# The layers' dense columns as three products of rounded parts

## The chip, the cores and the metric

The program runs on one core of a Trainium2 chip. The metric is the time of one execution on the device, in microseconds (us). Five engines take part: TensorE (PE; its weight loads are rows of their own, PEld), VectorE (DVE), ScalarE (ACT), GpSimd (POOL) and SyncE (SP), which issues nearly all the transfers from memory (DMA).

## What is computed

The reference is two layers of one model, a final norm, and then a block of a second model, all in fp32 with 256 tokens of 1024 features. The change concerns the two layers, and there the products of the normed tokens with columns of `w_in`:

```python
for layer in range(DEPTH):                      # DEPTH = 2
    h = rms_norm(x, norm1_g[layer])             # 256 x 1024
    sb = cols(SB_OFF, SB_COLS)                  # cols: h @ w_l[:, lo:lo + width]
    y_sb = stick_breaking_attention(...)
    y_rwkv, v_first = rwkv7_time_mix(cols(RWKV_OFF, RWKV_COLS), ...)
    y_moba = moba_attention(...)                # of cols(MOBA_OFF, MOBA_COLS)
    y_hgrn = hgrn2_mixer(...)                   # of cols(HGRN_OFF, HGRN_COLS)
    for n, y_n in enumerate((y_sb, y_rwkv, y_moba, y_hgrn)):
        gate = jax.nn.sigmoid(cols(GATE_OFF + n * D_MODEL, D_MODEL))
        merged += gate * (y_n @ w_branch[layer, n])
    x = x + merged @ w_out[layer]
    h2 = rms_norm(x, norm2_g[layer])
    x = x + (silu(h2 @ w_ffn_gate[layer]) * (h2 @ w_ffn_up[layer])) @ w_ffn_down[layer]
```

The columns are 768 for `sb`, 768 for `moba`, 1024 for `hgrn` and 4096 for the four gates; the 1024 of `rwkv` are computed before the others and aren't changed. They are 6656 columns a layer.

## The kernel before

Everything is written by hand: each engine has a program of its own, and semaphores order them. A tile is 128 partitions wide, so the 1024 features are 8 tiles of 128 x 256 (`x`, `B.h`).

**A unit** is what one visit to a PSUM bank makes: 128 columns for all 256 tokens (kind "c"), or 256 columns for 128 tokens (kinds "0" and "1", for the values of the attentions). It is 8 products, of 128x128 with 128x256, in fp32; the profile shows each fp32 product as two matmul rows. A layer has 52 units: 20 for the branches (`hq`, `hg`, `sq`, `sv`, `mq`, `mv`), then 32 for the gates. The generator `units` stops after every 4 products, so a unit is two half-units and a layer has 104.

**The order in a layer.** First come the RWKV columns (the loop over `RP`, matmuls of L1145), while VectorE makes the normed tiles `h` and the shifted `R.p`. Then the RWKV recurrence runs in 42 steps, each a few small matmuls with work of VectorE or ScalarE between them. `mix` puts half-units between the steps: `RW_PLAN` says how many follow each one (7, 3, 1, 4, 3, then mostly 1; 64 in all). The matmuls of these steps are those of L743 and L739 and some of L212, those of the units are L212 with `ring` among their operands. Steps on which the prediction rests: "kn" (the norm of the keys: VectorE makes `kk2`, PE sums, VectorE makes `kmax`, ScalarE takes Ln and Exp with two table loads, VectorE makes `rk` for the next step "bo"); "wc/we" (PE, then three exponentials on ScalarE, then VectorE makes `AR` and `KB`, then PE transposes `KB`); four steps M with one for L (VectorE masks what PE made); 24 steps that double an inverse in six levels; five steps of W, U and y; and the norm of `y`, whose variance VectorE makes, whose root ScalarE makes, and which PE transposes ("yT"). Then the branch product `b1`, and then the steps of `hgrn`, `stick` and `moba` by turns, with the other 40 half-units between them by `MX_PLAN`. After that PE does the other branch products, the output product (L1173) and the feed-forward part.

All engines run the same `mix` with the same plan, and each engine executes its own program strictly in order. On ScalarE the half-units are where it empties the bank of the unit before:

```python
for i in range(n):
    yield
    if i:
        done(i - 1)
    yield
```

**Loads.** SyncE fills three slots of 16 KB a partition in turn (`ring`); a slot is free when PE has used what was in it. Before the change a slot takes 512 columns (2048 KB) or 256 (1024 KB).

**The feed-forward part** (`split`, `group3`) already works in the way that the change brings to the units: ScalarE copies fp32 weights rounded to fp32r (`high_part`), VectorE subtracts that from the weights to make the low part (`low_part`), and PE makes three products in fp32r (high by high, high by low, low by high) in place of one in fp32. Its operands are named `rarena`.

Of the kernel before, what the change touches and what calls it, by code (L numbers as in the profile page):

```python
# [6 lines left out]
ALU = mybir.AluOpType  # L7
# [6 lines left out]
L = 2  # L14
# [6 lines left out]
IN1 = 7680  # L21
# [246 lines left out]
def build(nc, a, outs, coff, ooff, ocols):  # L268
    with ExitStack() as ctx:
# [9 lines left out]
        ring = ctx.enter_context(nc.sbuf_tensor("ring", [128, NSLOT, SLOT], F32))  # L279
# [62 lines left out]
        def pc(key, i=0, n=1):  # L342
# [40 lines left out]
        B.h = alloc(8, 256)  # L383
        B.tm = alloc(2, 256)
# [7 lines left out]
        B.hg = alloc(2, 256)  # L392
        mark = place["top"]
        R = Space()
        R.rp = alloc(8, 257)
        R.p = alloc(8, 256)
        R.r, R.k, R.v = R.p[:, 0:2, :], R.p[:, 2:4, :], R.p[:, 4:6, :]
        R.th = alloc(256)
        R.lw = alloc(2, 256)
        R.av = alloc(2, 256)  # L400
        R.sg = alloc(256)
        R.g = alloc(2, 256)
        R.M4 = alloc(8, 512)
        mm_ = flat(R.M4)
        R.vv = mm_[:, 0:256]
        R.vg = halves(mm_[:, 256:768])
        R.dv = halves(mm_[:, 768:1280])
        R.kk = alloc(2, 256)
# [7 lines left out]
        R.KB = alloc(2, 2, 256)  # L416
        R.em = alloc(2, 2)
# [8 lines left out]
        R.Wt = alloc(256)  # L426
        R.U = alloc(256)
# [4 lines left out]
        H = Space()  # L432
        H.key = alloc(2, 256)
        H.lf = alloc(2, 256)
        H.qd = alloc(2, 256)
# [123 lines left out]
        IN1 = [("hq", 2560, 512, "cccc"), ("hg", 3072, 512, "01cc"), ("sq", 0, 512, "cccc"), ("sv", 512, 256, "01"),  # L559
               ("mq", 1792, 512, "cccc"), ("mv", 2304, 256, "01")]  # L560
        gate_col = lambda n, ch: 3584 + 1024 * n + 512 * ch
# [50 lines left out]
        def sync_program(S):  # L612
# [19 lines left out]
            def units(l, c0, w, n):  # L632
                columns(f"{l}w{c0}", a["w_in"][l], 8, c0, w)
                for _ in range(n):
                    yield
                    yield

            def proj(l):
                for nm, c0, w, parts in IN1:
                    yield from units(l, c0, w, len(parts))  # L640

            def gate(l, n, ch):
                yield from units(l, gate_col(n, ch), 512, 4)
# [15 lines left out]
            for l in range(L):  # L659
# [8 lines left out]
                fill = [proj(l)] + [gate(l, n, ch) for n in (1, 0, 2, 3) for ch in range(2)]  # L668
# [49 lines left out]
        def tensor_program(PE):  # L718
# [31 lines left out]
            def units(l, nm, c0, w, parts):  # L750
                wt = halves(wslot(f"{l}w{c0}")[:, 0:8 * w], 8)
                PE.wait_ge(f"{l}w{c0}")
                o = 0
                for i, kind in enumerate(parts):
                    b = take("p", f"{l}{nm}{i}.ps", f"{l}{nm}{i}.out")
                    if kind == "c":
                        out = b[:, 0:256]
                        prs = [(wt[:, j, o:o + 128], B.h[:, j, :]) for j in range(8)]
                        o += 128
                    else:  # L760
                        t = int(kind)
                        out = b[:, 0:256]
                        prs = [(B.h[:, j, 128 * t:128 * t + 128], wt[:, j, o:o + 256]) for j in range(8)]
                        o += 256 if t == 1 else 0
                    PE.group(out, prs[0:4], end=False)
                    yield
                    PE.group(out, prs[4:8], first=False).then_inc(*PE(f"{l}{nm}{i}.ps"))
                    yield
                PE.mark(f"{l}w{c0}.used")

            def proj(l):
                for nm, c0, w, parts in IN1:
                    yield from units(l, nm, c0, w, parts)

            def gate(l, n, ch):
                yield from units(l, f"g{n}{ch}", gate_col(n, ch), 512, "cccc")
# [2211 lines left out]
```

## Time and profile before

| | us |
|---|---|
| median of 3 runs (lowest to highest) | 1977.25 (1975.52 to 1977.47) |
| the profiled execution, by its own time | 1975.95 |
| its span in the trace | 1974.2 |
| in it, first layer, from the first unit to the last step of the mixers | 42.6 to 315.8 |
| the same stretch of the second layer | 620.7 to 896.3 |

The profile is one execution. In the views below a time is in us from the start of the span. "idle" in a row is how long the engine stood before it, with what released it. TensorE is busy nearly everywhere in the two layers; the last quarter of the span, the second model's experts, waits for transfers. The granted clock of TensorE is a share of its full speed, 1.00 being 2.4 GHz and 0.50 being 1.2 GHz.

### The profile page before, as it was taken

To read this page: it belongs to the slowest core of one execution; us is meant where nothing else is said; L and a number is where in the kernel's file an instruction comes from. 1 tells how busy PE (TensorE), PEld (TensorE's weight loads), DVE (VectorE), ACT (ScalarE), POOL (GpSimd) and SP (SyncE) were. 2 spreads that over 40 slices of the span, in tenths; PEclk is the share of its full clock that TensorE was granted. 3 is DMA by queue.
4 is the path that set the end of the run, shared out by engine and by line. 5 is a ranking of instruction groups with operands and counts; after the bars stand their busy time and mean duration, and the time that the engine had idled before them with its cause. 6 is when DMAs were issued, how large, how long until landed. Compare 5 with 4: busy or idle time off the path is not lost.

```text
span 1974.2 us, 25562 instructions
## 1 busy us (share of the span) xinstructions
PE 1782.2 (90%) x11030; PEld 1388.9 (70%) x11030; DVE 746.4 (38%) x1220; ACT 513.6 (26%) x776; POOL 36.5 (2%) x42
## 2 busy tenths in 40 slices
PE   8999999999999999999999999999998975656655
PEld 6899887988898898888999998567887321111111
DVE  4532435455434532425666666332345100000001
ACT  2201221544342101211544464432542100000001
POOL 0000000100010000000100020000000000000000
PEclk9999999999999999999999999999999988888888
DMA  7221323677834221315554331401229999999997
GB/s 305 76 104 71 156 76 121 244 308 302 326 118 149 79 114 64 150 65 201 218 191 179 133 117 49 168 1 43 86 86 377 426 428 426 428 428 426 428 427 312
DMA packets 31073, 414.82 MB, mean 210 GB/s; under 512 B 3440, under 2 KB 3696, under 8 KB 4336
## 3 DMA queue, kind: packets, MB, share of 16 engines
q1 hardware_dynamic: 30528, 410.63, 52.2%
q10 hardware_dynamic: 432, 2.56, 0.3%
q8 instruction: 86, 1.41, 0.3%
q14 instruction: 27, 0.22, 0.0%
HBM read 412.13 MB, written 1.05 MB: 209 GB/s over the span
## 4 chain that ended last, share of the span: by engine, by line
PE 79%; DMA 15%; DVE 2%; ACT 1%; another core or an unknown queue 1%; issue 1%; POOL 0%; SPq 0%; DVEq 0%; ACTq 0%
PE ps L212 56%; DMA high<-in_w_e_gate_dram 7%; PE ps L743 7%; DMA high<-in_w_e_up_dram 5%; PE ps L1530 4%; PE ps L1145 3%; PE ps L1173 3%; DMA low<-in_w_e_up_dram 2%; PE ps L787 1%; DVE high L171 1%; ACT high L206 1%; PE ps L739 1%; PE ps L1545 1%; PE ps L1419 1%
## 5 line engine op out<-in xcount | busy, mean ns | idle before, releaser
L212 PE MATMUL ps<-high,ring 128*128 128x256 f32 (+1 forms) x2016 | 471.7, 386 | 0.9 <-ACT low L206 0.9
L212 PEld LDWEIGHTS ps<-rarena 128*128 128x128 f32 x3648 | 447.6, 192 | 16.3 <-DVE low L171 6.9
L212 PE MATMUL ps<-rarena 128*128 128x256 f32 (+1 forms) x3648 | 457.8, 287 | 0.0
L212 PEld LDWEIGHTS ps<-high,ring 128*128 128x128 f32 x2016 | 375.0, 190 | 65.6 <-issue 15.4
L206 ACT ACTIVATE high<-ps 128x256 f32<-128x256 f32 (+2 forms) x188 | 90.9, 483 | 623.3 <-PE ps L212 220.6
L171 DVE TENSOR_TENSOR rarena<-ring,rarena 128x2048 fp32r<-128x2048 f32 x76 | 168.4, 2215 | 106.9 <-ACT rarena L206 105.5
L206 ACT ACTIVATE rarena<-ring 128x2048 fp32r<-128x2048 f32 x76 | 140.4, 1847 | 243.5 <-PE ps L212 189.0
L171 DVE TENSOR_TENSOR high<-high,ps 128x512 f32<-128x512 f32 x52 | 35.7, 687 | 305.1 <-PE ps L1530 247.3
L1530 PE MATMUL ps<-high,low 128*32 128x512 f32 x592 | 90.1, 736 | 50.6 <-DMA high<-in_w_e_up_dram 33.8
L743 PEld LDWEIGHTS ps<-high 128*128 128x128 f32 (+1 forms) x992 | 104.0, 190 | 16.6 <-issue 8.0
L743 PE MATMUL ps<-high 128*128 128x128 f32 (+4 forms) x992 | 113.1, 291 | 1.9 <-DVE high L171 1.9
L206 ACT ACTIVATE low<-ps 128x256 f32<-128x256 f32 (+2 forms) x97 | 43.5, 448 | 267.7 <-PE ps L212 207.8
L212 PE MATMUL ps<-high 128*128 128x64 f32 (+5 forms) x512 | 111.5, 368 | 0.8 <-DVE high L193 0.8
L212 PEld LDWEIGHTS ps<-high 128*128 128x128 f32 (+2 forms) x512 | 83.5, 190 | 24.4 <-issue 13.4
L171 DVE TENSOR_TENSOR high<-ps,low 128x512 f32<-128x512 f32 (+1 forms) x47 | 30.1, 640 | 181.6 <-PE ps L1530 140.0
L1530 PEld LDWEIGHTS ps<-high,low 128*32 128x32 f32 x592 | 17.8, 122 | 112.5 <-DMA high<-in_w_e_up_dram 56.2
L171 DVE TENSOR_TENSOR high<-high 128x256 f32<-128x256 f32 (+9 forms) x108 | 59.1, 548 | 77.2 <-PE ps L743 53.7
L1530 PE MATMUL ps<-high 128*32 128x512 f32 x272 | 43.1, 764 | 31.4 <-DMA high<-in_w_e_down_dram 30.2
L1145 PE MATMUL ps<-low,ring 128*128 128x256 f32 x256 | 60.0, 394 | 8.6 <-DMA ring<-in_w_in_dram 8.6
L212 PE MATMUL ps<-low,ring 128*128 128x256 f32 x264 | 62.1, 395 | 4.5 <-issue 4.5
L206 ACT ACT_TABLE_LOAD x46 | 59.0, 1283 | 16.3 <-DVE high L176 13.3
L1145 PEld LDWEIGHTS ps<-low,ring 128*128 128x128 f32 x256 | 50.2, 198 | 16.9 <-DMA ring<-in_w_in_dram 8.6
(188 smaller groups left out, 1439.0 us busy)
## 6 DMA issues: line engine op xcount, KB each, us to landing
ring<-in_w_in_dram SPq DMA_DIRECT2D x34, 2048.0 KB, 7.5
ring<-in_w_ffn_up_dram SPq DMA_DIRECT2D x22, 2048.0 KB, 9.2
high<-in_w_e_up_dram SPq DMA_DIRECT2D x20, 2048.0 KB, 49.6
high<-in_w_e_gate_dram SPq DMA_DIRECT2D x17, 2048.0 KB, 47.7
high<-in_w_e_down_dram SPq DMA_DIRECT2D x17, 2048.0 KB, 50.4
ring<-in_w_mod_dram SPq DMA_DIRECT2D x12, 2048.0 KB, 8.2
ring<-in_w_e_down_dram SPq DMA_DIRECT2D x10, 2048.0 KB, 48.7
ring<-in_w_ffn_down_dram SPq DMA_DIRECT2D x8, 2048.0 KB, 8.4
```

Of the source, the lines that this page charges most:

```text
L171: return self.e.tensor_tensor(out, x, y, op)
L206: return self.e.activation(out, x, f, scale=scale, **kw)
L212: ins = self.e.matmul(out, l, r, start=first and i == 0, stop=end and i == n - 1)
L739: ins = PE.e.transpose(o, z, ident[0:k, 0:k])
L743: return PE.e.matmul(out, l, r, start=True, stop=True)
L787: ins = PE.e.matmul(b[32 * j:32 * j + 2, :], cc[:, 2 * kq + k, :], w[:, k, j, :], start=kq == 0 and k == 0, stop=kq == 3 and k == 1)
L1145: ins = PE.e.matmul(b[:, 0:256], w[:, j, 128 * m:128 * m + 128], B.xg[:, j, :], start=j == 0, stop=j == 7)
L1173: ins = PE.e.matmul(b[:, 0:256], w[:, j, 128 * m:128 * m + 128], B.mg[:, j, :], start=j == 0, stop=j == 7)
L1419: ins = PE.e.matmul(bs[i][:, 0:256], w[:, k, 128 * i:128 * i + 128], T.yT[:, k, :], start=k == 0, stop=k == 7)
L1530: ins = PE.e.matmul(bs[ch][32 * e_:32 * e_ + 32, :], lhs(k, e_), w[:, e_, 512 * ch:512 * ch + 512], start=k == 0, stop=k == 7)
L1545: ins = PE.e.matmul(banks[4 + 2 * t + ch][:, :], E.SGT[:, g_, 128 * t:128 * t + 128], E.y[:, 512 * ch:512 * ch + 512], start=g_ == 0, stop ...
```

## The change

Both operands of the units are split. `B.h` is rounded by ScalarE to `B.hh` and VectorE makes the rest, `B.hl`. Of the weights, ScalarE rounds the columns of one unit, two units ahead of its use, into the upper half of the slot (`high_weights`); GpSimd subtracts and writes the low part over the weights (`low_weights`); PE waits for GpSimd and makes three fp32r products where one fp32 product was. A load brings 256 columns, two units. The buffers of RWKV are laid over one another to make room (`R.p`, `R.th`, `R.lw` and others lie in `R.M4`), and those of hgrn move in front of them. The loads of the RWKV columns, the feed-forward part and everything after the layers stay.

```diff
@@ -276,7 +276,9 @@
-        ring = ctx.enter_context(nc.sbuf_tensor("ring", [128, NSLOT, SLOT], F32))
+        with nc.sbuf_tensor("ring", [128, NSLOT, SLOT], F32) as ring:
+            pass
+        rring = ctx.enter_context(nc.sbuf_tensor("rring", [128, NSLOT, SLOT], mybir.dt.float32r))
...
@@ -381,6 +383,8 @@
+        place["top"] -= 8 * 256
+        B.hl, B.hh = ralloc_low(8, 256), ralloc_low(8, 256)
...
         R.M4 = alloc(8, 512)
         mm_ = flat(R.M4)
+        R.p = mm_[:, 0:2048].rearrange("p (i n) -> p i n", i=8)
+        R.r, R.k, R.v = R.p[:, 0:2, :], R.p[:, 2:4, :], R.p[:, 4:6, :]
+        R.th, R.sg = mm_[:, 2048:2304], mm_[:, 2304:2560]
+        R.lw, R.av, R.kk = (halves(mm_[:, o:o + 512]) for o in (2560, 3072, 3584))
+        R.g = alloc(2, 256)
...
+        R.vg, R.dv = R.KB[:, 0, :, :], R.KB[:, 1, :, :]
...
+        GATES = [(f"g{n}{ch}", 3584 + 1024 * n + 512 * ch, "cccc") for n in (1, 0, 2, 3) for ch in range(2)]
+        UNITS = [(nm, i, kind, c0 + 256 * (i // 2), i % 2) for nm, c0, kinds in IN1 + GATES for i, kind in enumerate(kinds)]
+        raw_part = lambda ld: halves(wslot(ld)[:, 0:2048], 8)
+        rslot = lambda ld: rring[:, slot_of.get(ld, 0), :].bitcast(F32)
+        low_weights = lambda ld: halves(rslot(ld)[:, 0:2048], 8)
+        high_weights = lambda ld: halves(rslot(ld)[:, 2048:4096], 8)
+        unit_columns = lambda z: slice(128 * z, 128 * z + 128)
...
+            def units(l):
+                for nm, i, kind, c0, z in UNITS:
+                    if z == 0:
+                        columns(f"{l}w{c0}", a["w_in"][l], 8, c0, 256)
+                    yield
+                    yield
...
@@ -747,33 +747,23 @@
+            def units(l):
+                for u, (nm, i, kind, c0, z) in enumerate(UNITS):
+                    wl, wh = low_weights(f"{l}w{c0}"), high_weights(f"{l}w{c0}")
+                    PE.wait_ge(f"{l}u{u}.lo" if kind == "c" else f"{l}u{u + 1 - z}.lo")
...
                     if kind == "c":
-                        out = b[:, 0:256]
-                        prs = [(wt[:, j, o:o + 128], B.h[:, j, :]) for j in range(8)]
-                        o += 128
+                        o = unit_columns(z)
+                        prs = [(wh[:, j, o], wl[:, j, o], B.hh[:, j, :], B.hl[:, j, :]) for j in range(8)]
+                        o = unit_columns(int(kind))
+                        prs = [(B.hh[:, j, o], B.hl[:, j, o], wh[:, j, :], wl[:, j, :]) for j in range(8)]
+                    PE.group3(b[:, 0:256], prs[0:4], end=False)
+                    yield
+                    PE.group3(b[:, 0:256], prs[4:8], first=False).then_inc(*PE(f"{l}{nm}{i}.ps"))
+                    if z:
+                        PE.mark(f"{l}w{c0}.used")
+                    yield
...
-                PE.wait_ge(f"{l}h7")
-                fill = [proj(l)] + [gate(l, n, ch) for n in (1, 0, 2, 3) for ch in range(2)]
...
+            def gate_unit(l, nm, i):
...
+            def rounded(l, u):
+                nm, i, kind, c0, z = UNITS[u]
+                A.wait_ge(f"{l}w{c0}")
+                o = unit_columns(z)
+                high_part(f"{l}u{u}.hi", high_weights(f"{l}w{c0}")[:, :, o], raw_part(f"{l}w{c0}")[:, :, o])
+
+            def rounded_ahead(l, u):
+
+                kind, z = UNITS[u][2], UNITS[u][4]
+                if kind == "c":
+                    rounded(l, u)
+                elif z == 0:
+                    rounded(l, u)
+                    rounded(l, u + 1)
+
+            def units(l):
+                for u in range(len(UNITS)):
+                    yield
+                    if u:
+                        nm, i = UNITS[u - 1][0:2]
+                        (gate_unit if nm[0:2] in ("g0", "g1", "g2", "g3") else input_unit)(l, nm, i)
+                    if u + 2 < len(UNITS):
+                        rounded_ahead(l, u + 2)
+                    yield
+                gate_unit(l, *UNITS[-1][0:2])
...
                 for n in range(8):
+                    A.wait_ge(f"{l}h{n}")
+                    high_part(f"{l}h{n}.hi", B.hh[:, n, :], B.h[:, n, :])
                     if n in EARLY_STEPS[l]:
                         next(rw)
-                fill = [proj(l)] + [gate(l, n, ch) for n in (1, 0, 2, 3) for ch in range(2)]
+                rounded(l, 0)
+                rounded(l, 1)
...
+                def normed_tile(n):
+                    V.stt(B.h[:, n, :], x[:, n, :], pc(("norm1_g", l), n), B.rs, mul, mul).then_inc(*V(f"{l}h{n}"))
+
+                def low_tile(n):
+                    V.wait_ge(f"{l}h{n}.hi")
+                    low_part(B.hl[:, n, :], B.h[:, n, :], B.hh[:, n, :], f"{l}h{n}.lo")
+
+                normed_tile(0)
                 for n, i in enumerate(RP):
-                    V.stt(B.h[:, n, :], x[:, n, :], pc(("norm1_g", l), n), B.rs, mul, mul).then_inc(*V(f"{l}h{n}"))
+                    if n < 7:
+                        normed_tile(n + 1)
+                    low_tile(n)
                     V.wait_ge(f"{l}rp{i}.ps")
...
+            def units(l):
+                for u, (nm, i, kind, c0, z) in enumerate(UNITS):
+                    G.wait_ge(f"{l}u{u}.hi")
+                    raw, o = raw_part(f"{l}w{c0}"), unit_columns(z)
+                    G.tt(fr(low_weights(f"{l}w{c0}")[:, :, o]), raw[:, :, o], high_weights(f"{l}w{c0}")[:, :, o], ALU.subtract).then_inc(
+                        *G(f"{l}u{u}.lo"))
...
+    out["w_in"] = [column_blocks(w["w_in"][l], [256, 256, 256, 512] + 25 * [256]) for l in range(L)]
```

`raw` in the program of GpSimd is `raw_part`, the fp32 weights in the slot.

ScalarE's queue from the last tile of `h` over the step "kn" (table load, 128x512, table load, 128x512 are its Ln and Exp) to the first emptied banks (`high<-ps 128x256`); `rring<-ring` is the rounding of one unit:

```order
+L206 ACTIVATE rarena<-high 128x256
+L206 ACTIVATE rring<-ring 128x8x128 x2
 L206 ACT_TABLE_LOAD
 L206 ACTIVATE high<-high 128x512
 L206 ACT_TABLE_LOAD
 L206 ACTIVATE high<-high 128x512
-L206 ACTIVATE high<-ps 128x256 x2
+L206 ACTIVATE rring<-ring 128x8x128
+L206 ACTIVATE high<-ps 128x256
+L206 ACTIVATE rring<-ring 128x8x128
+L206 ACTIVATE high<-ps 128x256
+L206 ACTIVATE rring<-ring 128x8x128 x2
```

Two roundings (of units 0 and 1) stand ahead of the Ln and Exp of "kn", and the third (of unit 2) stands behind them.

TensorE's queue from the last RWKV column (L1135, before L1145) over "kn" (the first L743 128x512) and "bo" (the second); an order row counts an fp32 product once:

```order
-L1145 MATMUL ps<-low,ring 128x256 x8
-L212 MATMUL ps<-high,ring 128x256 x8
+L1135 MATMUL ps<-low,ring 128x256 x8
+L212 MATMUL ps<-rarena,rring 128x256 x24
 L743 MATMUL ps<-high,low 128x512
-L212 MATMUL ps<-high,ring 128x256 x20
+L212 MATMUL ps<-rarena,rring 128x256 x60
 L743 MATMUL ps<-high,low 128x512
```

The units stand where they stood, with three matmuls for one; unit 0 is ahead of "kn", and units 1, 2 and half of 3 are between "kn" and "bo".

GpSimd's queue between the sums for the first layer's two norms:

```order
-L171 TENSOR_TENSOR low<-low 128x256 x29
+L171 TENSOR_TENSOR low<-low 128x256
+L171 TENSOR_TENSOR rring<-ring,rring 128x8x128 x52
+L171 TENSOR_TENSOR low<-low 128x256 x14
+L171 TENSOR_TENSOR rring<-ring,rring 128x8x128 x52
+L171 TENSOR_TENSOR low<-low 128x256 x14
```

It gets 52 subtractions of 128x1024 in each layer.

## Rows read from the trace of the kernel before

**Rows 1.** The page, first part: busy time by engine.

```profile
PE 1782.2 (90%) x11030; PEld 1388.9 (70%) x11030; DVE 746.4 (38%) x1220; ACT 513.6 (26%) x776; POOL 36.5 (2%) x42
```

**Rows 2.** Windows: busy us of PE, PEld, DVE, ACT, POOL, clock, DMA.

```profile
100.00:200.00 100.00, 100.00 (x633) 91.79 (x632) 31.90 (x55) 9.59 (x21) 0.00 (x0) 1.00 0.25 92
```

**Rows 3.** Timeline, first layer, around "kn": start, us, engine, operation, count, idle before.

```profile
42.57 3.62 PE L212 MATMUL ps<-high,ring 128*128 128x256 f32 x16
45.44 0.69 DVE L171 TENSOR_TENSOR high<-high 128x512 f32<-128x512 f32 x1
47.15 8.80 PE L212 MATMUL ps<-high,ring 128*128 128x256 f32 x40
48.11 1.28 ACT L206 ACT_TABLE_LOAD   x1 [8.20 <-DVE high L176]
52.01 0.69 DVE L171 TENSOR_TENSOR high<-high 128x512 f32<-128x512 f32 x1 [3.96 <-ACT high L206]
54.36 1.01 DVE L181 SCALAR_TENSOR_TENSOR high<-high,col 128x256 f32<-128x256 f32 x2
55.79 1.02 PE L743 MATMUL ps<-high,low 128*128 128x512 f32 x2
```

**Rows 4.** Timeline of PE in the feed-forward part (fp32r, two jobs of 48).

```profile
385.15 11.78 PE L212 MATMUL ps<-rarena 128*128 128x256 f32 x96
396.86 1.90 PE L787 MATMUL ps<-ring,low 128*2 128x512 f32 x16
```

**Rows 5.** Groups by line and shape: busy us, mean ns | idle before.

```profile
L171 POOL TENSOR_TENSOR low<-low 128x1024 f32<-128x1024 f32 x1 | 2.3, 2342 | 9.8 <-ACT low L206 9.8
...
L206 ACT ACTIVATE rarena<-ring 128x1024 fp32r<-128x1024 f32 x6 | 6.4, 1060 | 17.7 <-PE ps L212 17.6
...
L171 DVE TENSOR_TENSOR rarena<-high,rarena 128x256 fp32r<-128x256 f32 x8 | 3.7, 468 | 1.4 <-ACT high L206 0.7
```

**Rows 6.** DMA issues: KB each, median us to landing.

```profile
ring<-in_w_in_dram SPq DMA_DIRECT2D x8, 1024.0 KB, 4.9
```

**Rows 7.** Timeline, second layer, around the first unit.

```profile
620.74 3.72 PE L212 MATMUL ps<-high,ring 128*128 128x256 f32 x16
620.84 0.98 ACT L206 ACTIVATE high<-ps,low 128x256 f32<-128x256 f32 x2 [8.54 <-PE ps L743]
```

**Rows 8.** Timeline, first layer, "wc/we" to M.

```profile
65.54 2.74 ACT L206 ACTIVATE high<-ps 128x512 f32<-128x512 f32 x5 [6.58 <-PE ps L743]
69.01 2.60 DVE L171 TENSOR_TENSOR high<-high 128x256 f32<-128x256 f32 x4
72.03 1.01 PEld L739 LDWEIGHTS ps<-cst,high 128*128 128x128 f32 x8
78.39 1.14 PE L743 MATMUL ps<-high 64*128 64x256 f32 x8
```

**Rows 9.** Timeline, first layer, the end of the M stage.

```profile
98.14 1.16 PE L743 MATMUL ps<-high 128*128 128x128 f32 x8 [0.68 <-DVE high L171]
```

**Rows 10.** Timeline: a GpSimd operation beside one of VectorE, four places.

```profile
360.83 2.29 DVE L171 TENSOR_TENSOR rarena<-ring,rarena 128x2048 fp32r<-128x2048 f32 x1
360.86 2.84 POOL L171 TENSOR_TENSOR low<-low 128x256 f32<-128x256 f32 x1 [346.13 <-ACT low L206]
...
364.72 0.72 POOL L171 TENSOR_TENSOR low<-low 128x256 f32<-128x256 f32 x1 [1.01 <-ACT low L206]
364.81 0.42 DVE L181 SCALAR_TENSOR_TENSOR low<-ps,low 128x256 f32<-128x256 f32 x1
...
1158.38 0.73 POOL L171 TENSOR_TENSOR high<-high 128x256 f32<-128x256 f32 x1
1158.61 0.79 DVE L181 SCALAR_TENSOR_TENSOR low<-low 128x256 f32<-128x256 f32 x1 [3.61 <-ACT low L206]
```

**Rows 11.** Timeline and windows, the end of the first layer's fill.

```profile
318.09 3.65 PE L212 MATMUL ps<-low,ring 128*128 128x256 f32 x8 [2.27 <-issue]
...
318.50:319.00 0.50, 0.50 (x2) 0.39 (x2) 0.00 (x0) 0.00 (x0) 0.00 (x0) 0.50 0.00 0
```

More of the change, by code:

```diff
@@ L392, in build @@
         B.hg = alloc(2, 256)
+        H = Space()
+        H.key = alloc(2, 256)
+        H.lf = alloc(2, 256)
+        H.qd = alloc(2, 256)
         mark = place["top"]
@@ L426, in build @@
         R.Wt = alloc(256)
+        R.vv = R.Wt
         R.U = alloc(256)
@@ L431, in build @@
         gx = [B.gates] + [alloc(8, 256) for _ in range(2)]
[L432 to L435, printed above, removed]
         H.ST = alloc(8, 128)
@@ L667, in sync_program @@
                     table["par"] = (s_par, 32)
-                fill = [proj(l)] + [gate(l, n, ch) for n in (1, 0, 2, 3) for ch in range(2)]
+                fill = [units(l)]
                 mix([none(RW_STEPS)], fill, RW_PLAN, False)
@@ L1153, in tensor_program @@
                         next(rw)
-                PE.wait_ge(f"{l}h7")
-                fill = [proj(l)] + [gate(l, n, ch) for n in (1, 0, 2, 3) for ch in range(2)]
+                PE.wait_ge(f"{l}h7.lo")
+                fill = [units(l)]
                 for _ in range(2):
@@ L1609, in input_unit @@
                     evict(l, nm, i, B.mv[:, i, :])
[L1611 to L1626 removed]
+            def gate_unit(l, nm, i):
+                n, ch = int(nm[1]), int(nm[2])
+                buf = B.mg if n == 1 else gx[max(n - 1, 0)]
+                evict(l, nm, i, buf[:, 4 * ch + i, :], Tanh, scale=0.5)
+            def rounded(l, u):
[12 more added lines that the diff above has]
+                for u in range(len(UNITS)):
+                    yield
+                    if u:
[3 more added lines that the diff above has]
+                        rounded_ahead(l, u + 2)
+                    yield
+                gate_unit(l, *UNITS[-1][0:2])
             def none(n):
@@ L1809, in scalar_program @@
                 for n in range(8):
+                    A.wait_ge(f"{l}h{n}")
+                    high_part(f"{l}h{n}.hi", B.hh[:, n, :], B.h[:, n, :])
                     if n in EARLY_STEPS[l]:
                         next(rw)
-                fill = [proj(l)] + [gate(l, n, ch) for n in (1, 0, 2, 3) for ch in range(2)]
+                rounded(l, 0)
+                rounded(l, 1)
+                fill = [units(l)]
                 mix([rw], fill, RW_PLAN, False)
@@ L2075, in proj @@
             def proj(l):
-                for nm, c0, w, parts in IN1[:2]:
-                    yield from late(len(parts), lambda i, nm=nm: input_unit(l, nm, i))
+                for nm, c0, kinds in IN1[:2]:
+                    yield from late(len(kinds), lambda i, nm=nm: input_unit(l, nm, i))
             def modulation():
@@ L2801, in pool_program @@
             G.mark("0n1.fold")
+            units(0)
             folded("0n2", F.sq)
             folded("1n1", B.gates)
+            units(1)
             folded("1n2", F.sq)
@@ L2883, in pack_weights @@
     out = {}
-    out["w_in"] = [column_blocks(w["w_in"][l], [512, 256, 512, 256, 256, 512, 256] + 10 * [512]) for l in range(L)]
+    out["w_in"] = [column_blocks(w["w_in"][l], [256, 256, 256, 512] + 25 * [256]) for l in range(L)]
     out["w_branch"] = [[rows_on_partitions(w["w_branch"][l, n], 2) for n in range(4)] for l in range(L)]
```

52 lines of the change are left out of this document (2 added, 50 removed).

## The prediction

> **What bounds the kernel now.** I read the page first: TensorE is busy 90% of the span, GpSimd 2% [rows 1]. The windows of 100 us say the same of the layers: from 100 to 200 TensorE is busy all of the time at clock 1.00, VectorE a third of it and ScalarE a tenth [rows 2]. So the layers last as long as TensorE's queue, and the other engines work in its shade. How deep the shade is, the timeline shows. At the step "kn", VectorE's last operation ends at 46.13, TensorE then gives 5 half-units (47.15 to 55.79) while ScalarE's Ln and Exp with two table loads run to 52.01 and VectorE finishes `rk` at 55.37, 0.4 us before TensorE asks for it [rows 3]. In this place cover and chain are equally long. That is where I look for losses.
>
> **What TensorE saves.** Five fp32 half-units take 55.79 - 47.15 = 8.64, so one takes 1.728 [rows 3]. In the feed-forward part 96 fp32r matmuls take 396.86 - 385.15 = 11.71, or 0.122 each; a half-unit of 12 will take 1.464 [rows 4]. The difference is 0.264, and 2 layers x 104 half-units give **-54.9 us**, if nobody makes TensorE wait.
>
> **What is added.** For each unit ScalarE rounds 128x1024 (1.06) and GpSimd subtracts 128x1024 (2.34; this row is of a plain tile, the new one is read in 8 runs) [rows 5]. A unit on TensorE will take 2.93, so in steady state both keep up; 52 x 2.34 = 122 us of GpSimd a layer lie under some 270. VectorE's eight low tiles (0.47 each) lie in the RWKV columns, where it waits for TensorE anyway: nothing, and 3.7 a layer without that cover. Their roundings on ScalarE (8 x 0.5) lie there too. The laid-over buffers cost nothing: what shares `R.M4` is read before the first M in each queue. Loads of 1024 KB land in 4.9 [rows 6]; a slot is refilled while two units (5.9 or more) run, so they arrive in time, with 1 us to spare in a run of units without steps. A miss would cost under 1 us at each of a few loads; I count none.
>
> What isn't free is the order. A unit needs, one after the other, ScalarE's rounding and GpSimd's subtraction: 1.06 + 2.34 and hand-overs, 3.5. ScalarE does that two units ahead, but behind what its queue holds.
>
> 1. First unit. In the first layer the roundings follow the last tile of `h`; I get 1.4 us of waiting by the same sum. In the second, ScalarE is at the attention to `vg` until 620.84 + 0.98 = 621.82, so unit 0 is ready at 625.3, where TensorE wanted it at 620.74: 4.6 [rows 7]. Together **+6.0**.
> 2. Unit 2 at "kn". The queue has its rounding behind Ln and Exp. ScalarE begins these 2.0 after `kk2` (48.11 against 46.13) and ends them 3.9 later [rows 3]; with 3.5 behind it unit 2 is ready 9.4 after TensorE begins "kn". TensorE has only "kn" (1.0) and unit 1 (2.93) until then: 5.5 in each layer, **+11.0**. This is what the old cover hid: all five half-units could run under ScalarE's work, now two can.
> 3. In the rest of the burst (18 half-units up to M) the same happens smaller: pairs of units "01" wait for the second low part, and unit 7's rounding stands behind the three exponentials of "wc/we", whose result TensorE's transposes need too (from 65.54 to 72.03, of which four half-units now cover 5.9) [rows 8]: 2 a layer, **+4.0**.
> 4. M stage. From 78.39 to 98.14 VectorE has no pause to speak of, and TensorE waits for it at the end [rows 8, 9]. Its 7 faster half-units gain nothing: 7 x 0.264, **+3.7**. In the 24 steps of the doubling VectorE has 0.5 to 1 us to spare a step, so the saving there is whole.
> 5. Norm of `y`: ScalarE does Ln and Exp before it rounds unit 30: 2.3 a layer, **+4.6**.
> 6. The mixers: ScalarE has a block of exponentials and table loads of some 6 us once a layer, and softmax exponentials twice; the three half-units that a rounding is ahead (4.4 us) don't cover them: 3.6 a layer, **+7.2**.
> 7. Clock. The one wait over 2 us inside a layer (2.27) was followed by clock 0.50, and 8 matmuls took 3.48 to the next row, not 1.73 [rows 11]. I expect four such waits; each costs 1.75, half of it under a wait that comes anyway: **+3.5**.
>
> Sum so far +40.0, and the kernel would take 1975.95 - 54.9 + 40.0 = 1961.
>
> **VectorE and GpSimd at once.** A GpSimd subtraction of 0.7 us took 2.84 when it began 0.03 after one of VectorE that ran 2.29; and an operation of VectorE of 128x256 took 0.79 when it began 0.23 after a GpSimd one, where two of the kind take 1.01 by themselves [rows 3, 10]. Where one of VectorE's inputs is in PSUM, both took what they take alone (0.42 and 0.72) [rows 10]. So two SBUF inputs on VectorE and a GpSimd operation exclude each other, whole operations at a time. The Trainium skill (SBUF — State Buffer, Who interferes with whom) says just this, that the loser blocks for the whole operation, and adds VectorE's copies and tensor-scalars from SBUF to SBUF in a two-port mode; no row here shows the latter. By that page the change moves elementwise work to the one engine that can stop VectorE.
>
> Now GpSimd's operation is 2.34 and there are 104. The doubling reads PSUM in each operation, and is safe. But "kn" to `rk` has four operations with two SBUF inputs and tensor-scalars between, exactly while GpSimd has units 2 to 5 to do: one gets through for each of these, so 3.4 us become about 11, of which TensorE feels 3.3. `kk2` is delayed by 1.9 (first layer) and 0.8 (second) by units 0 and 1, `KB` (seven such operations, two of GpSimd between them) by some 4, of which 3 are felt beyond item 3; less what replaces waits counted above this is 7.4 and 6.4. The M stage ends in four operations of this kind: one meeting, and two of tensor-scalars, less VectorE's pauses: 3 a layer. Norm of `y` 1.4, softmax of moba 3 a layer. Sum 13.8 + 6 + 2.8 + 6 = **+28.6** as the upper bound, nothing as the lower. Copies and tensor-scalars are 13 of it; since every row of an SBUF-to-SBUF operation beside GpSimd shows the wait, I count them too. I take 25, as some meetings fall where VectorE would wait anyway: 1961 + 25 = **1986**. The execution profiled is 1.3 below the median, which I ignore.
>
> **The rivals.**
> - *No exclusion that matters* (faster): meetings fall into VectorE's pauses, which are two thirds of its time. Then the waits of items 1 to 7 are all: 1961, between 1950 and 1970. For it speaks the light load of VectorE, against it that the chains that matter run with GpSimd by construction.
> - *TensorE stays the bound throughout* (faster): of the list only item 1 stays, 1975.95 - 54.9 + 6 = 1927. Against it stands the order of ScalarE's queue, which item 2 reads off.
> - *GpSimd is the slow one* (slower): its operation on 8 runs takes longer than the plain one, which no row bounds from above; from the 2.93 of a unit on it decides the pace of the bursts. At 4.7, twice the row, units 2 to 8 lose 7 x 1.8 and the mixers' 20 units, which have about 4.3 each, lose 8: with item 2's 2.3 more, 23 a layer, 2030; at 3.5 some 5 a layer, 1996.
> - *It cancels out*: half the exclusion and less of items 3 to 6: 1973 to 1981.
>
> **How the numbers follow.** Less than 0.2% (4 us) is about what a measurement of this kernel can't tell from no change. Exclusion as worked out, 1981 to 2000: 0.42. Cancels out: 0.12. No exclusion that matters: 0.26. TensorE the bound: 0.08. GpSimd slow, 2000 to 2030: 0.12. So faster 0.34, same 0.12, slower 0.54. The range leaves out the lowest case and the end of the highest: 1948 to 2008; the likeliest case's own is 1976 to 2000.
>
> **What the new profile would show.** Item 2: TensorE idle some 5 us a layer shortly after "kn", released by GpSimd, with ScalarE's rounding behind a table load. Exclusion: VectorE's 128x256 and 128x512 operations with two SBUF inputs at 1 to 2.5 us where they overlap GpSimd's, those with PSUM unchanged; VectorE's busy time up by tens of us. Steady saving: a half-unit between doubling steps at 1.46 to 1.50. GpSimd's mean near 2.4. TensorE's idle time in the two layers would be 50 to 70 us. If that idle is under 25, or the half-unit isn't near 1.46, or GpSimd's mean is over 3, I am wrong in the step named.

## The result and the profile after

The changed kernel takes 1992.97 us (median of 8 runs, 1984.97 to 1999.23) against 1977.36 before: a ratio of 1.0077, with a 95% interval of 1.0062 to 1.0091. Slower by 15.6 us; predicted were 1986 and slower as the likeliest. The execution profiled took 1992.94, with a span of 1991.1.

The page of the changed kernel, busy time by engine:

```profile
PE 1745.0 (88%) x11862; PEld 1393.2 (70%) x11862; DVE 847.4 (43%) x1236; ACT 630.8 (32%) x896; POOL 289.0 (15%) x146
...
L171 POOL TENSOR_TENSOR rring<-ring,rring 128x1024 fp32r<-128x1024 f32 x104 | 252.7, 2429 | 344.0 <-ACT rring L206 338.8
```

Beside [rows 1] TensorE is busy 37 us less and VectorE 101 us more, though VectorE got only 16 operations more, of some 0.45 each. GpSimd's mean is 2.43 (the plain tile in [rows 5] took 2.34).

The place of [rows 3] in the changed kernel, timeline of the first layer from "kn" to the product that reads `rk`:

```profile
53.42 1.12 PE L743 MATMUL ps<-high,low 128*128 128x512 f32 x2 [1.60 <-DVE high L171]
53.98 3.42 PE L212 MATMUL ps<-rarena,rring 128*128 128x256 f32 x24
...
55.34 1.28 ACT L206 ACT_TABLE_LOAD   x1 [8.10 <-DVE high L176]
...
59.24 0.69 DVE L171 TENSOR_TENSOR high<-high 128x512 f32<-128x512 f32 x1 [3.97 <-ACT high L206]
59.30 1.06 ACT L206 ACTIVATE rring<-ring 128x1024 fp32r<-128x1024 f32 x1
59.97 2.97 DVE L177 TENSOR_SCALAR high<-high,col,low 128x256 f32<-128x256 f32 x2
...
60.43 10.16 POOL L171 TENSOR_TENSOR rring<-ring,rring 128x1024 fp32r<-128x1024 f32 x4 [9.31 <-ACT rring L206]
...
62.83 6.93 PE L212 MATMUL ps<-rarena,rring 128*128 128x256 f32 x36 [5.44 <-POOL rring L171]
62.97 2.89 DVE L171 TENSOR_TENSOR high<-high 128x512 f32<-128x512 f32 x1
...
65.89 4.99 DVE L181 SCALAR_TENSOR_TENSOR high<-high,col 128x256 f32<-128x256 f32 x2
...
70.93 1.13 PE L743 MATMUL ps<-high,low 128*128 128x512 f32 x2 [1.16 <-DVE high L181]
...
73.32 4.43 PE L212 MATMUL ps<-rring,rarena 128*128 128x256 f32 x36
77.59 1.95 PE L743 MATMUL ps<-low,high 128*128 128x128 f32 x16
```

Three things are to be seen. Unit 2 is rounded at 59.30, behind Ln and Exp; TensorE stands 5.44 for it. VectorE's chain from 59.24 to `rk` takes 11.64, where it took 3.36 before, while GpSimd does four subtractions. And after the wait 36 matmuls take 6.93, where 36 more of the kind take 4.27 a little later (73.32 to 77.59).

The waits of TensorE in the changed kernel, first layer (who waits, for whom: total us, times, longest):

```profile
PE ps L743 <- DVE high L171: 11.6, 4, 5.9
PE ps L212 <- POOL rring L171: 10.5, 5, 5.4
...
PE ps L739 <- DVE high L171: 2.4, 1, 2.4
PE ps L739 <- DVE high L176: 2.1, 2, 1.7
PE ps L743 <- DVE high L181: 1.2, 1, 1.2
```

And in the second layer:

```profile
PE ps L212 <- POOL rring L171: 9.9, 5, 5.4
PE ps L743 <- DVE high L171: 5.1, 2, 4.8
PE ps L212 <- DVE high L176: 5.0, 1, 5.0
...
PE ps L743 <- DVE high L181: 1.9, 1, 1.9
```

With the small ones and the 2.28 at branch 0 these are 31.1 and 29.3 us, against 3.3 and 3.8 before: 53 us more. The row of 5.0 is unit 0 of the second layer. It names VectorE, but what the unit waits for in the code is GpSimd's subtraction, which began at 641.45, and TensorE went on at 644.19. The windows from the first unit to the end of the doubling, and of the stretch behind branch 0 that answers to [rows 11] (us, then busy us of PE, PEld, DVE, ACT, POOL, clock, DMA):

```profile
48.73:71.00 22.27, 14.06 (x87) 12.96 (x87) 16.61 (x13) 12.40 (x16) 12.12 (x5) 0.85 0.25 92
71.00:94.80 23.80, 19.77 (x158) 18.71 (x158) 10.74 (x13) 10.21 (x15) 9.11 (x4) 1.00 0.34 112
94.80:124.25 29.45, 19.77 (x134) 16.57 (x133) 27.59 (x31) 5.77 (x8) 13.13 (x6) 0.92 0.25 89
124.25:191.39 67.14, 67.14 (x561) 67.14 (x562) 25.77 (x39) 17.32 (x24) 26.66 (x12) 0.96 0.25 84
...
331.99:362.09 30.10, 30.10 (x124) 26.46 (x125) 18.90 (x28) 1.79 (x3) 0.00 (x0) 0.79 0.36 139
```

The windows of the kernel before that answer to the last row and to the one of 124.25:

```profile
98.14:170.06 71.92, 71.92 (x464) 66.97 (x465) 25.74 (x39) 4.60 (x12) 0.00 (x0) 1.00 0.27 100
...
318.09:343.68 25.59, 25.59 (x124) 22.62 (x125) 18.91 (x28) 1.79 (x3) 0.00 (x0) 0.93 0.44 166
```

The stretch behind branch 0 has the same instructions as before, without a wait in it; it took 25.59 at clock 0.93 there and takes 30.10 at 0.79 here. The M stage (94.80 to 124.25) takes 29.45, where it took 19.75. In the 24 doubling steps (124.25 to 191.39) VectorE isn't slowed: GpSimd is busy 26.66 us there, and VectorE's 39 operations, most of them with an input in PSUM, take 25.77 where they took 25.74.

### The profile page after: what moved, and what is told of

Read it like the earlier page. It is cut to its first block, busy times and chain, and to the rows that moved or that the text cites. A ratio compares the mean times of both kernels' runs of the same rounds, so it can differ in the third digit from the quotient of the medians.

```text
span 1991.1 us, 27735 instructions
## 1 busy us (share of the span) xinstructions
PE 1745.0 (88%) x11862; PEld 1393.2 (70%) x11862; DVE 847.4 (43%) x1236; ACT 630.8 (32%) x896; POOL 289.0 (15%) x146
## 4 chain that ended last, share of the span: by engine, by line
PE 69%; DMA 13%; DVE 10%; ACT 3%; another core or an unknown queue 2%; issue 1%; POOL 1%; SPq 0%; DVEq 0%; ACTq 0%
PE ps L212 48%; PE ps L743 6%; PE ps L1520 6%; DVE high L171 5%; DMA high<-in_w_e_up_dram 5%; DMA high<-in_w_e_gate_dram 5%; PE ps L1163 3%; DMA low<-in_w_e_down_dram 2%; PE ps L1135 2%; ACT high L206 2%; PE ps L777 1%; DVE high L181 1%; DMA low<-in_late_dram 1%; PE ps L739 1%
## 5 line engine op out<-in xcount | busy, mean ns | idle before, releaser
L212 PE MATMUL ps<-rarena,rring 128*128 128x256 f32 x2208 | 304.1, 294 | 25.4 <-POOL rring L171 20.4
L212 PEld LDWEIGHTS ps<-rarena,rring 128*128 128x128 f32 x2208 | 281.9, 196 | 36.8 <-POOL rring L171 20.9
L171 POOL TENSOR_TENSOR rring<-ring,rring 128x1024 fp32r<-128x1024 f32 x104 | 252.7, 2429 | 344.0 <-ACT rring L206 338.8
L212 PE MATMUL ps<-high,ring 128*128 128x256 f32 (+1 forms) x544 | 130.7, 393 | 0.9 <-ACT low L206 0.9
L743 PE MATMUL ps<-high 128*128 128x128 f32 (+4 forms) x992 | 117.3, 295 | 15.0 <-DVE high L171 15.0
L171 DVE TENSOR_TENSOR high<-high 128x256 f32<-128x256 f32 (+9 forms) x108 | 103.7, 960 | 53.7 <-PE ps L743 34.0
L212 PEld LDWEIGHTS ps<-high,ring 128*128 128x128 f32 x544 | 102.3, 190 | 23.9 <-issue 9.8
L743 PEld LDWEIGHTS ps<-high 128*128 128x128 f32 (+1 forms) x992 | 103.5, 194 | 21.6 <-DVE high L171 16.3
L206 ACT ACTIVATE rring<-ring 128x1024 fp32r<-128x1024 f32 x104 | 110.2, 1059 | 21.9 <-DMA ring<-in_w_in_dram 15.8
L171 POOL TENSOR_TENSOR low<-low 128x256 f32<-128x256 f32 (+2 forms) x31 | 29.1, 940 | 546.0 <-ACT low L206 353.1
```

The source lines that it names most:

```text
L171: return self.e.tensor_tensor(out, x, y, op)
L206: return self.e.activation(out, x, f, scale=scale, **kw)
L212: ins = self.e.matmul(out, l, r, start=first and i == 0, stop=end and i == n - 1)
L743: return PE.e.matmul(out, l, r, start=True, stop=True)
```

## The experiments

All are compared with the kernel before, measured beside them at 1977.5 to 1978.0. The changed kernel was not measured again beside them. A difference between two experiments, or to the changed kernel, is one of two medians, each with an interval of some 3 us, and is good to some 4 us; where it is smaller than that, only the traces speak for it.

**The change taken apart, products last.** The first four build the change up with the old fp32 products, so that nothing is saved and each cost shows by itself. In a0_layout ScalarE, GpSimd and VectorE do nothing for these columns. From a1_scalar on the rounding is there, and TensorE waits for a pair's two events ahead of the pair's last half-unit, so that the slot isn't handed back too early (in a1_scalar these are ScalarE's `.hi`). a3_waited keeps the changed kernel's wait for the low part ahead of each unit (the second line of the diff below), and the roundings and subtractions of h. The core of the edits:

```diff
-                    wl, wh = low_weights(f"{l}w{c0}"), high_weights(f"{l}w{c0}")
-                    PE.wait_ge(f"{l}u{u}.lo" if kind == "c" else f"{l}u{u + 1 - z}.lo")
+                    wt = raw_part(f"{l}w{c0}")
+                    PE.wait_ge(f"{l}w{c0}")
-    prs = [(wh[:, j, o], wl[:, j, o], B.hh[:, j, :], B.hl[:, j, :]) for j in range(8)]
+    prs = [(wt[:, j, o], B.h[:, j, :]) for j in range(8)]
+                    if z: PE.wait_ge(f"{l}u{u - 1}.lo", f"{l}u{u}.lo")
...
-    G.tt(fr(low_weights(...)[:, :, o]), raw[:, :, o], high_weights(...)[:, :, o], ALU.subtract)
+    G.tt(fr(high_weights(...)[:, :, o]), raw[:, :, o], high_weights(...)[:, :, o], ALU.subtract)
```

> The changed kernel with its loads of 256 columns and its tighter RWKV buffers, but with the old fp32 products (8 matmuls a half-unit) straight from the loaded weights and from h: nothing is rounded on ScalarE, nothing subtracted on GpSimd or VectorE for these columns. The output is the reference's. My theory, which costs loads and buffers at nothing: 1977 within 2 us, TensorE's idle time in the layers as before. Rival (a new wait for loads, or for a buffer that now lies over another): 1981 or more, with waits released by a DMA or by the engine that holds the buffer.

Measured: 1977.21, ratio 0.9996 (0.9987 to 1.0004). Loads of 256 columns and the tighter buffers cost nothing, as expected.

> As a0_layout, and ScalarE rounds the weights of each unit into the free half of the slot, 52 operations of 1.06 us a layer in the places that the changed kernel gives them. Nobody reads the result, the products stay fp32; a slot is handed back only after its two roundings. My theory: ScalarE has room and the cost is small, 0 to 4 us over a0_layout, from the three exponentials and the evictions that stand behind a rounding. Rival (ScalarE's extra 55 us a layer are what costs): 10 us or more.

Measured: 1980.13, ratio 1.0014 (1.0002 to 1.0027): 2 to 3 us. VectorE's chain at "kn" has its old durations; the timeline of a1_scalar:

```profile
52.72 0.86 DVE L177 TENSOR_SCALAR high<-high,col,low 128x256 f32<-128x256 f32 x2
53.62 0.69 DVE L171 TENSOR_TENSOR high<-high 128x512 f32<-128x512 f32 x1
54.35 1.01 DVE L181 SCALAR_TENSOR_TENSOR high<-high,col 128x256 f32<-128x256 f32 x2
```

> As a1_scalar, and GpSimd subtracts for each unit (128x1024, its result unused, written over the rounded half). The products don't wait for it, only the slot's return does. My theory (a GpSimd operation and one of VectorE with its inputs in SBUF exclude each other): 15 to 25 us over a1_scalar, on VectorE's chains from kn to rk, KB, and the M stage; VectorE's SBUF operations there at 1 to 2.5 us each, its busy time up by some 80 us. Rival (no exclusion that matters): within 3 us of a1_scalar.

Measured: 2026.93, ratio 1.0249 (1.0231 to 1.0266): 47 us over a1_scalar, two to three times what I expected. The same operations of VectorE in a2_gpsimd, with GpSimd's beside them:

```profile
54.72 2.98 DVE L177 TENSOR_SCALAR high<-high,col,low 128x256 f32<-128x256 f32 x2
57.73 2.87 DVE L171 TENSOR_TENSOR high<-high 128x512 f32<-128x512 f32 x1
60.64 4.93 DVE L181 SCALAR_TENSOR_TENSOR high<-high,col 128x256 f32<-128x256 f32 x2
65.62 2.07 PE L743 MATMUL ps<-high,low 128*128 128x512 f32 x2 [6.00 <-DVE high L181]
...
55.19 10.10 POOL L171 TENSOR_TENSOR rring<-ring,rring 128x1024 fp32r<-128x1024 f32 x4 [9.31 <-ACT rring L206]
```

Nobody waits for GpSimd's result here, so this is the exclusion alone: four operations of GpSimd, and one or two of VectorE get through for each. TensorE stands 18 us in the first layer for VectorE and 20 in the second, where it stood 1.0 and 1.5 in a1_scalar, and no wait of it ends with GpSimd. So some 35 of the 47 us are waits for VectorE; most of the rest is a lower granted clock behind them (TensorE's busy time times the missing clock, over windows of 1 us, is 21.6 us up to 960, against 6.7). GpSimd's operations are the only work added to a1_scalar, so that they cost this is shown. That it comes by whole operations is read off the rows above.

> As a2_gpsimd, and the eight tiles of h are rounded and subtracted as well, and TensorE waits before each unit for GpSimd's subtraction as in the changed kernel, still with fp32 products. The only difference to the changed kernel is then 8 fp32 matmuls in place of 12 fp32r for each half-unit. My theory (the order of ScalarE's queue at kn and at the first unit makes TensorE wait): 20 to 27 us over a2_gpsimd, of which 11 at kn; and the changed kernel is 45 to 55 below this one. Rival (the waits come only because the products are shorter): within 8 us of a2_gpsimd.

Measured: 2027.20, ratio 1.0249 (1.0229 to 1.0268). On balance the waits for the low part cost nothing on top. TensorE now stands 4.84 for unit 2 and only 0.89 at the product of `rk`, where it stood 6.00: one wait has taken the place of the other, as both end with GpSimd's burst. The 20 to 27 us that I expected on top aren't there. The time is the rival's, though not for its reason, since unit 2 is waited for with the old products too. The changed kernel is 34 us below this one; I expected 45 to 55.

**The order of ScalarE's queue.** b1_late is the first piece of this diff, b2_kn the second (the rounding of units 2 and 3 at its old place is then skipped), b3_both has both:

```diff
-                    A.wait_ge("par", "dl")
+                    A.wait_ge("dl")
...
                     if n in EARLY_STEPS[l]:
+                        if l == 0: A.wait_ge("par")
                         next(rw)
...
+                A.wait_ge(f"{l}kk2")
+                rounded(l, 2)
+                rounded(l, 3)
                 A.wait_ge(f"{l}kn.ps")
                 A.wait_ge(f"{l}kmax")
```

> The changed kernel, but ScalarE waits for the parameters that arrive last (late) only ahead of the step that reads them, at the fifth tile of h in the first layer, no longer ahead of its first rounding of h. In the changed kernel's profile ScalarE stands 6.07 us at this wait, VectorE 4.96 behind it, TensorE 2.86. My theory: 4 to 5 us less than the changed kernel's 1993, about 1988.5. Rival (the eight low tiles themselves hold VectorE up, 8 x 0.45): less than 1.5 us.

Measured: 1988.31, ratio 1.0052 (1.0039 to 1.0065): 4.7 less than the changed kernel. The traces say the same: unit 0 starts at 44.27 here and at 48.73 there. These rows of the changed kernel's timeline are what goes, with a wait of TensorE for ScalarE of 1.25 behind them:

```profile
23.85 0.92 ACT L206 ACTIVATE rarena<-high 128x256 fp32r<-128x256 f32 x2 [6.07 <-DMA low<-in_late_dram]
24.30 0.42 DVE L171 TENSOR_TENSOR rarena<-high,rarena 128x256 fp32r<-128x256 f32 x1 [4.96 <-ACT rarena L206]
...
25.31 7.17 PE L1135 MATMUL ps<-low,ring 128*128 128x256 f32 x32 [2.86 <-DVE high L171]
```

> The changed kernel, but ScalarE rounds units 2 and 3 before Ln and Exp of the step kn, as soon as VectorE has written kk2, instead of behind them. GpSimd can then subtract both while VectorE waits for Exp anyway. The order theory (item 2 of the prediction): the wait for unit 2 (5.44 us in each layer) goes, and with two GpSimd operations fewer beside VectorE's chain from kn to rk the wait at bo doesn't take its place: 1977 to 1984. Rival, from the run in which nothing waits for the subtraction and TensorE still stood 6.0 and 7.2 at bo: the wait moves on to bo, 1988 or more.

Measured: 1982.38, ratio 1.0043 (1.0022 to 1.0064): 10.6 less than the changed kernel. Its eight times lie in two groups, five at 1979.69 to 1982.78 and three at 1992.32 to 1994.59, so the median says less than its digits; the trace is one of the first group. In it the wait for unit 2 is gone in both layers, but the rival was half right: at the product of `rk` TensorE stands 5.1 and 4.9 instead of 1.2 and 1.9. All its waits together fell by some 8 us in the two layers. In b3_both, which has the same edit, TensorE stands there too, since units 4 and 5 are still subtracted beside VectorE's chain:

```profile
49.84 4.93 POOL L171 TENSOR_TENSOR rring<-ring,rring 128x1024 fp32r<-128x1024 f32 x2 [3.41 <-ACT rring L206]
...
56.94 4.92 POOL L171 TENSOR_TENSOR rring<-ring,rring 128x1024 fp32r<-128x1024 f32 x2 [2.17 <-ACT rring L206]
57.20 4.93 DVE L181 SCALAR_TENSOR_TENSOR high<-high,col 128x256 f32<-128x256 f32 x2
...
62.19 2.07 PE L743 MATMUL ps<-high,low 128*128 128x512 f32 x2 [5.15 <-DVE high L181]
```

> Both edits of b1_late and b2_kn. If they are independent: the sum of the two gains, 1973 to 1980.

Measured: 1977.35, ratio 1.0004 (0.9992 to 1.0017). The two gains add up (4.7 + 10.6 against 15.6), as far as these medians can tell.

**GpSimd's share.**

> The changed kernel, but GpSimd subtracts only the first of a unit's eight rows of blocks (128x128 instead of 128x1024), and the products of the other seven read the rounded part where they read the low part: TensorE, ScalarE and all waits stay, GpSimd's work falls to an eighth. Left out is the low part of seven eighths of the weights. Exclusion theory: nearly all of the 47 us that GpSimd's operations cost when nobody waited for them goes, and 2 us of latency a unit with them: 1940 to 1955. Rival (ScalarE's order is the larger part, items 1 to 3 and 6 of the prediction, 28 us of which only some 7 are GpSimd's duration): 1965 or more.

```diff
-    G.tt(fr(low_weights(...)[:, :, o]), raw[:, :, o], high_weights(...)[:, :, o], ALU.subtract)
+    G.tt(fr(low_weights(...)[:, 0:1, o]), raw[:, 0:1, o], high_weights(...)[:, 0:1, o], ALU.subtract)
```

Measured: 1938.12, ratio 0.9797 (0.9785 to 0.9810), 55 us less than the changed kernel and a little better than I expected. VectorE is busy 761.4 us, near its time before. ScalarE's order still costs 3.55 at unit 2 here. By the traces, the waits of TensorE and its loss to the clock fall by 39 and 17 us. So of what the change loses, the larger part comes from the length of GpSimd's work: as a lock on VectorE, or as a late result. This run doesn't tell the two apart.

> The changed kernel, but GpSimd does each unit's subtraction in four operations of 128x256 (0.71 each in the profiles, 2.84 for a unit in place of 2.43) instead of one of 128x1024. Same work, same waits, and a unit is ready a little later. Exclusion by whole operations: VectorE waits for at most one piece, 0.7 in place of 2.4, and gets a turn between two pieces; of the 47 us that GpSimd cost, a good half goes: 1958 to 1972. Rival (what hurts is GpSimd's late result, or GpSimd's traffic as such and not the length of an operation): 1990 or more, since a unit's low part comes 0.4 us later.

```diff
+    for j in range(0, 8, 2):
+        G.tt(fr(low_weights(...)[:, j:j + 2, o]), raw[:, j:j + 2, o], high_weights(...)[:, j:j + 2, o], ALU.subtract)
```

Measured: 1992.84, ratio 1.0072 (1.0059 to 1.0085): no gain. My expectation was wrong for the time, which is the rival's; it was right in that VectorE gets its turn between two pieces. VectorE's chain to `rk`, and GpSimd's burst beside it, in the timeline of c1_pieces:

```profile
59.34 1.34 DVE L177 TENSOR_SCALAR high<-high,col,low 128x256 f32<-128x256 f32 x2
...
60.72 1.17 DVE L171 TENSOR_TENSOR high<-high 128x512 f32<-128x512 f32 x1
61.92 1.70 DVE L181 SCALAR_TENSOR_TENSOR high<-high,col 128x256 f32<-128x256 f32 x2
...
59.81 13.44 POOL L171 TENSOR_TENSOR rring<-ring,rring 128x256 fp32r<-128x256 f32 x16 [6.49 <-ACT rring L206]
```

The waits of TensorE in the first layer of c1_pieces:

```profile
PE ps L212 <- POOL rring L171: 21.1, 12, 6.6
PE ps L743 <- DVE high L171: 5.7, 2, 5.4
```

VectorE's chain takes 5.0 and not 11.6. But a unit now takes GpSimd 13.44 / 4 = 3.36, more than the 2.85 that TensorE needs for one (2 x 1.423, from the 36 matmuls above). Four pieces at the 0.72 of [rows 10] would be 2.9, so the number of operations accounts for most of the rise from 2.43; the rest I put down to GpSimd now waiting for VectorE, which no run separates. TensorE's waits for GpSimd double to 21.1 in the first layer. What the one engine is spared the other pays.

> The four pieces of c1_pieces on top of the two edits of b3_both (rounding of h ahead of the late parameters, units 2 and 3 rounded before Ln and Exp of kn). If the causes are separate: b3_both's 1977 less what c1_pieces gains on the changed kernel, 1942 to 1957. Rival (the wait at bo, 5 us a layer in b3_both, stays): 1960 or more.

Measured: 1975.34, ratio 0.9984 (0.9975 to 0.9994), 2.0 below b3_both, which these medians can't tell from nothing. The 20 to 35 us of my expectation are not there. The time is in the rival's range, but not for its reason: the wait at the product of `rk` did fall, to 1.8 and 1.7, and TensorE's waits for GpSimd rose from 5.6 and 4.4 to 16.0 and 18.7.

> b3_both, but VectorE subtracts instead of GpSimd, for all 52 units of a layer (about 1.2 us each by its 128x1024 rows): units 0 to 3 in VectorE's pauses ahead of kn, the others one or two half-units after their rounding. GpSimd then never runs beside VectorE in the dense columns. Exclusion theory: 127 us more work on VectorE cost less than 253 us on GpSimd, since nothing is waited for beyond its own 1.2: 1950 to 1968, and worst in the M stage, where VectorE is the bound (3 units, 3.7 us a layer). Rival (VectorE becomes the bound in the doubling and the mixers too): 1977 or more.

```diff
+    def unit_low(l, u):
+        V.wait_ge(f"{l}u{u}.hi")
+        low_part(low_weights(...)[:, :, o], raw_part(...)[:, :, o], high_weights(...)[:, :, o], f"{l}u{u}.lo")
```

The function is VectorE's. Measured: 1988.97, ratio 1.0048 (1.0035 to 1.0062): above b3_both, a miss, and in the rival's range. The timelines of TensorE and VectorE in c3_vector at the end of the M stage:

```profile
105.71 2.93 PE L212 MATMUL ps<-rring,rarena 128*128 128x256 f32 x12 [9.94 <-DVE rring L171]
...
103.47 0.86 DVE L177 TENSOR_SCALAR high<-high,low 128x256 f32<-128x256 f32 x2
104.43 1.22 DVE L171 TENSOR_TENSOR rring<-ring,rring 128x1024 fp32r<-128x1024 f32 x1
```

A subtraction takes VectorE 1.22, half of GpSimd's time, but one stands behind VectorE's whole M stage, and in the mixers one wait of 6.68 appears. VectorE's queue has its own order. Other places for the subtractions in it were not tried.

> As c3_vector for the first ten units of a layer (up to the M stage), GpSimd in whole operations for the other 42. The chains from kn to M are then free of GpSimd, the M stage is not. Exclusion theory: 1952 to 1966; the waits at bo (5 us a layer) and at the transposes of KB (2.4) fall under 1.5 each, those of the M stage (5.9 and 4.8) stay. Rival (VectorE's own subtractions delay its chain just as much): 1972 or more.

Measured: 1960.39, ratio 0.9909 (0.9895 to 0.9924): 33 us below the changed kernel, 17 below b3_both, whose two edits it has as well, and 17 below the kernel before. The timeline of c4_split, the chain to `rk`:

```profile
53.11 0.86 DVE L177 TENSOR_SCALAR high<-high,col,low 128x256 f32<-128x256 f32 x2
54.01 0.69 DVE L171 TENSOR_TENSOR high<-high 128x512 f32<-128x512 f32 x1
54.74 1.01 DVE L181 SCALAR_TENSOR_TENSOR high<-high,col 128x256 f32<-128x256 f32 x2
55.80 1.12 PE L743 MATMUL ps<-high,low 128*128 128x512 f32 x2 [0.84 <-DVE high L181]
```

All durations are the old ones. VectorE's own subtractions lie in the pauses where it waits for Exp or for TensorE. The waits of the M stage stay (4.6 and 7.3). One part of the expectation failed: the wait at the transposes of `KB` is 2.1 in each layer, not under 1.5. The subtraction itself is also shorter on VectorE, 1.22 and not 2.4, so the 17 us are the lock and the late result together.

## Why the prediction was right, and where it wasn't

The forecast came out of a saving, seven items of order and the exclusion. What it said the profile would show is there: GpSimd's mean is 2.43, a half-unit between doubling steps takes 1.50 (129.97 to 131.47), and TensorE stands 60 us in the two layers. By its own steps:

- **What TensorE saves**: I took 0.264 a half-unit from long runs of matmuls. In the changed kernel three half-units take 77.59 - 73.32 = 4.27, or 1.423 each, hand-over included, against 1.728 in [rows 3]: 0.305, and 63 us instead of 54.9. This is one of the shortest groups, though. From the first unit, its wait taken in, to the product of branch 0 the two layers take 275.5 and 277.8 us before (42.57 to 318.09, 620.74 to 898.58) and 284.7 and 280.4 after (47.31 to 331.99, 639.20 to 919.55). With the waits and the loss to the clock taken off, that is a saving of some 59 us, 0.285 a half-unit.
- **Item 1**: 1.42 and 4.99 us, against 1.4 and 4.6. But the edit I costed at nothing, rounding h, cost 4.7 at the start: not VectorE's eight operations, which I had named, but ScalarE's first rounding behind a wait for parameters (b1_late). I had looked for what hides the operations and not at what stood ahead of them in ScalarE's queue.
- **Item 2**: 5.44 and 5.45, against 5.5 each. b2_kn shows the cause: with the rounding ahead of Ln and Exp the wait is gone.
- **Item 3**: one wait of 1.63 a layer, against 2. It is the one for unit 7: ScalarE rounds that at 81.88, behind the exponentials of "wc/we", and TensorE goes on at 85.42. The waits for a pair's second low part, which the item counted too, don't appear as waits of their own.
- **Item 4 and the exclusion in the M stage**: 9.7 and 2.0 us longer in the two layers, against 4.9 each. At the end of the stage one of VectorE's 128x1024 operations takes 3.25 instead of 1.22 in both layers, and TensorE stands 5.87 and 4.79. What the first layer has besides is a run of tiny operations ahead of M, which the second doesn't have: VectorE was through them in 2.9 us before (76.05 to 78.98) and takes 10.4 here (93.84 to 104.25), and TensorE stands 3.81 for them. The prediction had overlooked them.
- **Item 5**: 0.24 and not 2.3. I had counted two units of cover; six half-units run there and suffice.
- **Item 6 with the softmax**: some 5 us of waits a layer, against 6.6.
- **Exclusion from "kn" to M**: VectorE's chain took 11.64 where I wrote "about 11"; TensorE felt 1.2 and 1.9 of it besides item 2 (I had 3.3), 1.6 at "kn" in the first layer and nothing new there in the second (1.9 and 0.8), and 2.4 at the transposes of `KB` (3). My statement that tensor-scalars are stopped as well, which no row of before showed, holds: two that took 0.86 take 2.97. By the Trainium skill (SBUF — State Buffer, Who interferes with whom) this is a mode with two ports and an exclusive lock; the traces agree that VectorE waits for whole operations of GpSimd, and ports they can't show. The Trainium skill says in the same section that the order of issue decides who blocks. The trace of the changed kernel agrees: GpSimd's subtraction that began at 118.60, 0.17 after one of VectorE of 1.22, took 3.25.
- **Item 7, the clock**: mis-sized, the largest error. I expected four slow stretches for 3.5 us. Adding TensorE's busy time times the missing clock over windows of 1 us gives 25.7 us in the two layers and the stretch behind branch 0, against 4.9 before: some 21 us. There are eight new waits of 2 us or more, not four, and behind seven of them TensorE's next matmuls take up to twice their time (6.93 against 4.27 above); behind the eighth, the 2.41 at 89.95, the clock stays at 1.00, while behind one of only 1.81 it falls (24 matmuls take 4.62 from 261.69 on), and behind another of 1.81 it doesn't (3.11 from 851.53 on). And the stretch behind branch 0 in the first layer lost 4.5 us with no wait of its own beyond the one that it had before.

So 53 us of waits, 21 of clock and 4.6 at the start stand against 59 saved, and the tail ran 2.5 us shorter (a wait for GpSimd of 3.01 that became 0.84). That makes 17, as was measured between the profiled spans; it has to, since the 59 were worked out from the same times. Beside the forecast: waits 53 against 61.5 (items 1 to 6 with 36.5, exclusion 25), a saving of 59 against 55, clock 21 against 3.5, start 4.6 against nothing, tail 2.5 less. The differences come to +7, which is the way from 1986 to 1993. The direction and most of the places were foreseen. That the number is so near is in part luck: of the 22 us missing at the clock and the start, 15 were made up for by waits put too high and a saving and a tail put too low.

One thing in the prediction was wrong in kind. It added order and exclusion as if they were separate. The exclusion alone, with the old products, makes TensorE wait 35 us more (a2_gpsimd), where the prediction had 28.6 at the most, and waiting for the low part adds nothing to that (a3_waited). Both come from the same bursts of GpSimd and in part lie over one another; take one away (b2_kn) and part of the other appears. Which of the two an individual us belongs to isn't settled; that the length of GpSimd's operations is behind about 55 us, waits and clock together, b4_eighth shows.

## What to carry to other kernels

That an engine is idle doesn't make work for it free: look at what stands ahead of it in the queues that feed it, and at which other engine it locks while it runs. For GpSimd beside VectorE, list VectorE's SBUF-to-SBUF operations on the chain that TensorE waits for, and put GpSimd's work beside VectorE's PSUM reads, as in the doubling steps here, or in its pauses; splitting it only moved the wait (c1_pieces). And count the clock: seven of the eight long new waits cost TensorE again after they had ended.

## What was not expected of the hardware

- Tiny operations are stopped like large ones: three tensor-scalars of 128x2 took 4.82 us from the first to the last beside GpSimd (0.58 in the trace of before). They stand in the first layer's run ahead of M.
- The lock works both ways: GpSimd's 128x1024 subtraction took 3.25 at 118.60 in the changed kernel, beside VectorE's 128x1024 ones, and VectorE's next one 3.25 as well instead of 1.22.
- The changed kernel's times spread over 14 us in its 8 runs, those of the kernel before over 5 in the 8 beside them; why isn't known.
